# Gate and up tiles of a feed-forward chunk multiplied together, alternating between two PSUM banks

## The chip, the cores and the metric

The kernel runs on one core of a Trainium2 chip. The metric is the device time of one execution in microseconds (us), from the first to the last instruction with what lies around them. The engines that matter here are TensorE (PE in the profile, its weight loads PEld), ScalarE (ACT), VectorE (DVE) and SyncE (SP), which issues the loads of the weights.

## The reference, cut to what matters

The program is a four-layer block followed by a two-layer block over 256 tokens of width 1024, in fp32. Between attention, convolution and gating stages stand 12 feed-forward stages, all of this form (8 in the first block, 4 in the second, where gate and up lie side by side in one matrix):

```
D_MODEL = 1024;  D_FF = 2816;  SEQ = 256
x = x + 0.5 * (silu(rms_norm(x, g) @ w_gate) * (rms_norm(x, g) @ w_up)) @ w_down
```

## The kernel before

**Tiles.** Every weight matrix is read in tiles of 128 partitions x 2048 fp32 values, 1 MB each, 543 in all. A tile goes through three buffers of one slot number: `raw` (filled by a DMA), `w_hi` (ScalarE's rounding of raw to fp32r, L511) and `w_lo` (VectorE's raw minus w_hi, L835). There are RING = 3 slots; tile n uses slot n mod 3. Each product is made of three fp32r matmuls (`matmul3`, L1466 to L1468): high by high, high by low, low by high.

**A feed-forward stage.** The 2816 inner columns are cut in 11 chunks of 256. A chunk has a gate tile and an up tile (8 slices of 128 rows by 256 columns: 2 x 8 x 3 = 48 matmuls each, of 256 output columns, into one of the four `up` banks per tile) and a down tile (2 x 2 x 2 x 3 = 24 matmuls of 512 output columns, into the four `acc` banks, six into one bank and then six into the next). The order of tiles in a stage, the same on all engines, is: gate 0, up 0, gate 1, up 1, down 0, gate 2, up 2, down 1, ..., gate 10, up 10, down 9, down 10. A norm stage stands before each, and TensorE fills part of it with 18 matmuls on constants.

**What sets the order.** The order on each engine is written out, and semaphores tie them:

- TensorE, `ffn` and `gate_up`: before each tile it waits for `lo_ready` (one count per tile, from L835) and for a free bank (`bank_free`). The last matmul of a tile increments `tile_used`. A down tile also waits for `hlo_ready`, the low part of the product of its chunk.
- ScalarE, `ffn` / `chunk`: it waits for `tile_used` of the gate tile n, converts tile n+3 (`w_hi`, L511), does silu of the gate's bank (L571), waits for `tile_used` of the up tile n+1, converts tile n+4, makes the high part of the product (L564), waits for the down tile, converts its successor.
- VectorE, `ffn` / `chunk`: it waits for `tile_used` and `hi_ready` and makes `w_lo` of tile n+3, the same for tile n+4, then gate times up (L934), releases the two banks, makes the low part of the product (L924), then `w_lo` of the down tile's successor.
- SyncE loads tile n+3 into `raw` as soon as `w_lo` of tile n is made.

The first two and the last two tiles of a stage need one more remark. A stage begins with two chunks without a down tile between them, so up 1 (tile 3) takes the slot of gate 0 (tile 0). A stage ends with two down tiles; down 10 (tile 32) takes the slot of gate 10 (tile 29). At the very first stage, tile 0 is converted before the norm's outputs and tiles 1 and 2 after them.

Of the kernel before, what the change touches and what calls it, by code (L numbers as in the profile page):

```python
# [14 lines left out]
P = 128  # L15
TOK = 256
NT = TOK // P
D = 1024
KD = D // P
# [3 lines left out]
RING = 3  # L23
CW = 256
# [88 lines left out]
def build(nc, A, out, plan=None):  # L113
    plan = plan or full_plan()
    with ExitStack() as ctx:
        def sb(name, shape, dt=F32):
            return ctx.enter_context(nc.sbuf_tensor(name, shape, dt))

        def sem(name):
            return ctx.enter_context(nc.semaphore(name))  # L120
# [5 lines left out]
        w_hi = [sb(f"w_hi{i}", [P, TILE], F32R) for i in range(RING)]  # L126
        w_lo = [sb(f"w_lo{i}", [P, TILE], F32R) for i in range(RING)]

        xT_hi = sb("xT_hi", [P, KD, TOK], F32R)
        xT_lo = sb("xT_lo", [P, KD, TOK], F32R)  # L130
# [102 lines left out]
        up = [ctx.enter_context(nc.psum_tensor(f"up{i}", [P, 512], F32)) for i in range(4)]  # L233
# [8 lines left out]
        tile_used = sem("tile_used")  # L242
# [82 lines left out]
        def tview(buf, nk, n):  # L325
            return buf[:, 0:nk * n].rearrange("p (k n) -> p k n", k=nk)
# [1132 lines left out]
        def _(pe):  # L1459
# [4 lines left out]
            def matmul3(ps, lh, ll, rh, rl, start, stop):  # L1464

                pe.matmul(ps, lh, rh, start=start, stop=False)  # L1466
                pe.matmul(ps, lh, rl, start=False, stop=False)  # L1467
                return pe.matmul(ps, ll, rh, start=False, stop=stop)  # L1468

            def take_bank():  # L1470

                if credit[0]:
                    credit[0] -= 1
                else:
                    pe.wait_ge(bank_free, seen.next(bank_free))
                banks[0] += 1
                return (banks[0] - 1) % 4
# [6 lines left out]
            def up_matmuls(n, b):  # L1484

                wh, wl = tview(w_hi[n % RING], KD, CW), tview(w_lo[n % RING], KD, CW)
                for m in range(2):
                    for k in range(KD):
                        if k % 2 == 0:
                            next_pair()  # L1490
                        last = matmul3(up[b][:, m * TOK:(m + 1) * TOK], wh[:, k, m * P:(m + 1) * P],
                                       wl[:, k, m * P:(m + 1) * P], xT_hi[:, k, :], xT_lo[:, k, :],
                                       k == 0, k == KD - 1)
                last.then_inc(tile_used, 1)
# [46 lines left out]
            def next_pair():  # L1541

                if pairs_to_come[0]:
                    pe.wait_ge(xlo_ready, seen.next(xlo_ready))
                    pairs_to_come[0] -= 1
# [17 lines left out]
            def down(n, c, start, stop):  # L1563
                pe.wait_ge(lo_ready, seen.next(lo_ready))
                pe.wait_ge(hlo_ready, seen.next(hlo_ready))
                down_matmuls(n, hT_hi[:, c % 2], hT_lo[:, c % 2], start, stop)
# [116 lines left out]
            def ffn(s, n0):  # L1683
                def gate_up(n, c, b, loop=False):
                    for j in range(2):
                        pe.wait_ge(lo_ready, seen.next(lo_ready))
                        if loop:
                            pe.wait_ge(bank_free, seen.next(bank_free))
                        else:
                            assert take_bank() == (b + j) % 4  # L1690
                        up_matmuls(n + j, (b + j) % 4)

                b = banks[0] % 4
                gate_up(n0, 0, b)
                gate_up(n0 + 2, 1, b + 2)
                down(n0 + 4, 0, True, False)
                with pe.Fori(0, 4) as i:
                    seen.enter(i, [(lo_ready, 6), (bank_free, 4), (hlo_ready, 2)])
                    gate_up(n0 + 5, 2, b, True)
                    down(n0 + 7, 1, False, False)  # L1700
                    gate_up(n0 + 8, 3, b + 2, True)
                    down(n0 + 10, 2, False, False)
                    seen.leave(4)
                banks[0] += 16
                gate_up(n0 + 29, 10, b)
                down(n0 + 31, 9, False, False)
                down(n0 + 32, 10, False, True)
# [293 lines left out]
            for k in range(KD):  # L2001
                last = pe.transpose(up[3][:, k * G_ROWS:(k + 1) * G_ROWS], g_rows[:, k * P:(k + 1) * P],
                                    ident[0:G_ROWS, 0:G_ROWS])
# [191 lines left out]
```

## Time and profile before

| | |
|---|---|
| device time, median of 2 runs | 3684.26 us (3683.72 to 3684.81) |
| span of the profiled execution | 3684.0 us |
| TensorE busy | 3532.3 us (96%), 24279 matmuls, as many weight loads |
| VectorE busy | 1845.2 us (50%) |
| ScalarE busy | 1549.9 us (42%) |
| DMA | 576.08 MB, mean 156 GB/s; a 1 MB tile lands 4.8 to 5.2 us after its issue |
| mean granted TensorE clock | 0.966 of full speed |

The profiled execution lies within 0.3 us of the median of the runs, so it can stand for them. Busy time of TensorE is the union of matmuls that overlap in their pipeline: a matmul of 256 columns is shown with 0.28 us and one of 512 with 0.39 us, while the next begins before it ends. How fast it goes is read from the distance between starts. A group `line engine operation out<-in` names the buffer without its number, so `up` stands for any of four banks.

### The profile page before, as it was taken

How to read it: one execution, taken by the hardware profiler on the slowest of the kernel's cores; microseconds unless marked ns; L12 is line 12 of the kernel's file. 1: busy time of each engine (PE TensorE's matmuls, PEld its weight loads, DVE VectorE, ACT ScalarE, POOL GpSimd, SP SyncE). 2: the span in 40 equal slices, each digit the busy share in tenths (PEclk: the TensorE clock that was granted, in tenths of full speed). 3: DMA queues.
4: the chain of work that ended last, by engine and by line, in shares of the span. 5: the costliest groups of instructions: out<-in, count | busy, mean ns of one | idle time of the engine just before them, and what ended most of it. 6: DMA issues, size and time to landing. Idle time of an engine off the chain costs nothing.

```text
span 3684.0 us, 57759 instructions
## 1 busy us (share of the span) xinstructions
PE 3532.3 (96%) x24279; PEld 3261.1 (89%) x24279; DVE 1845.2 (50%) x2276; ACT 1549.9 (42%) x1836; POOL 161.6 (4%) x253
## 2 busy tenths in 40 slices
PE   8999999859999999999999999999999999999998
PEld 8999999748999899998999899878998998878997
DVE  4455454564454554444554545534545545434544
ACT  4344444334443443433343344355444443455443
POOL 0000000020000000000000000032000000131000
PEclk9999999979999999999999999879999999789999
DMA  6554555414555445555455455513454455413552
GB/s 210 184 166 166 185 168 184 148 35 152 184 170 183 165 149 188 164 184 171 156 171 182 148 183 174 164 35 104 163 186 156 162 189 158 127 49 113 191 184 101
DMA packets 452308, 576.08 MB, mean 156 GB/s; under 512 B 44650, under 2 KB 393937, under 8 KB 452013
## 3 DMA queue, kind: packets, MB, share of 16 engines
q1 hardware_dynamic: 449612, 566.71, 46.7%
q0 software_dynamic: 2384, 6.63, 0.6%
q8 instruction: 124, 2.03, 0.2%
q10 hardware_dynamic: 144, 0.35, 0.0%
q14 instruction: 44, 0.35, 0.0%
HBM read 571.53 MB, written 1.08 MB: 155 GB/s over the span
## 4 chain that ended last, share of the span: by engine, by line
PE 89%; DVE 7%; ACT 3%; issue 1%; DMA 0%; DVEq 0%; POOL 0%; SPq 0%; ACTq 0%; POOLq 0%
PE up L1466 20%; PE up L1468 19%; PE up L1467 19%; PE acc L1466 7%; PE acc L1467 7%; PE acc L1468 7%; DVE w_lo L835 2%; PE acc L1535 2%; ACT w_hi L511 2%; PE acc L1585 1%; PE up L1858 1%; PE up L1526 1%; PE acc L1592 1%; PE acc L1586 1%; DVE xT_lo L867 0%
## 5 line engine op out<-in xcount | busy, mean ns | idle before, releaser
L835 DVE TENSOR_TENSOR w_lo<-raw,w_hi 128x2048 fp32r<-128x2048 f32 x543 | 1244.4, 2292 | 1371.7 <-ACT w_hi L511 1368.8
L511 ACT ACTIVATE w_hi<-raw 128x2048 fp32r<-128x2048 f32 x543 | 1038.0, 1913 | 1262.5 <-PE up L1468 1206.1
L1466 PE MATMUL up<-xT_hi,w_hi 128*128 128x256 f32 x5392 | 1535.1, 285 | 16.6 <-DVEq L1315 10.2
L1467 PE MATMUL up<-xT_lo,w_hi 128*128 128x256 f32 x5392 | 1530.3, 284 | 0.0
L1468 PE MATMUL up<-xT_hi,w_lo 128*128 128x256 f32 x5392 | 1530.2, 284 | 0.0
L1466 PEld LDWEIGHTS up<-xT_hi,w_hi 128*128 128x128 f32 x5392 | 1039.3, 193 | 30.2 <-issue 18.7
L1467 PEld LDWEIGHTS up<-xT_lo,w_hi 128*128 128x128 f32 x5392 | 1039.3, 193 | 4.6
L1468 PEld LDWEIGHTS up<-xT_hi,w_lo 128*128 128x128 f32 x5392 | 1039.2, 193 | 0.0
L1466 PE MATMUL acc<-w_hi,hT_hi 128*128 128x512 f32 x1216 | 476.3, 392 | 15.7 <-DVE hT_lo L924 15.7
L1467 PE MATMUL acc<-w_lo,hT_hi 128*128 128x512 f32 x1216 | 474.7, 390 | 0.0
L1468 PE MATMUL acc<-w_hi,hT_lo 128*128 128x512 f32 x1216 | 473.2, 389 | 0.0
L1466 PEld LDWEIGHTS acc<-w_hi,hT_hi 128*128 128x128 f32 x1216 | 228.8, 188 | 65.3 <-issue 21.6
L564 ACT ACTIVATE hT_hi<-prod 128x512 fp32r<-128x512 f32 x144 | 91.0, 632 | 433.9 <-DVE prod L934 392.7
L1468 PEld LDWEIGHTS acc<-w_hi,hT_lo 128*128 128x128 f32 x1216 | 228.3, 188 | 48.6
L1467 PEld LDWEIGHTS acc<-w_lo,hT_hi 128*128 128x128 f32 x1216 | 228.9, 188 | 42.0
L924 DVE TENSOR_TENSOR hT_lo<-prod,hT_hi 128x512 fp32r<-128x512 f32 x144 | 99.8, 693 | 100.9 <-ACT hT_hi L564 100.9
L1466 PE MATMUL up<-w_hi,xT_hi 128*128 128x512 f32 (+3 forms) x292 | 103.2, 353 | 19.0 <-DVEq L1088 11.4
L2038 POOL TENSOR_SCALAR units<-units,rsum 128x256 f32<-128x256 f32 x80 | 67.2, 851 | 1069.8 <-DVE rsum L1026 1069.8
L523 ACT ACTIVATE xT_hi<-acc,gains 128x256 fp32r<-128x256 f32 x163 | 68.4, 471 | 88.6 <-PE acc L1535 76.7
L605 ACT ACTIVATE units<-units,nmax 128x256 f32<-128x256 f32 (+1 forms) x192 | 80.5, 421 | 55.5 <-DVE nmax L1018 51.2
L1468 PE MATMUL up<-w_hi,xT_lo 128*128 128x512 f32 (+3 forms) x292 | 102.4, 351 | 0.0
L1467 PE MATMUL up<-w_lo,xT_hi 128*128 128x512 f32 (+3 forms) x292 | 102.4, 351 | 0.0
(282 smaller groups left out, 2535.1 us busy)
## 6 DMA issues: line engine op xcount, KB each, us to landing
raw<-in_ffn_gate SPq DMA_DIRECT2D x88, 1024.0 KB, 5.1
raw<-in_ffn_up SPq DMA_DIRECT2D x88, 1024.0 KB, 5.2
raw<-in_ffn_down SPq DMA_DIRECT2D x88, 1024.0 KB, 4.8
raw<-in_ffn_wi SPq DMA_DIRECT2D x88, 1024.0 KB, 5.0
raw<-in_ffn_wo SPq DMA_DIRECT2D x44, 1024.0 KB, 4.8
raw<-in_w_in SPq DMA_DIRECT2D x44, 1024.0 KB, 5.0
raw<-in_conv_w_in SPq DMA_DIRECT2D x24, 1024.0 KB, 5.1
raw<-in_w_branch SPq DMA_DIRECT2D x12, 1024.0 KB, 5.0
```

The lines of the kernel that those rows point to most:

```text
L511: nc.scalar.activation(w_hi[n % RING][:], raw[n % RING][:], ACT.Copy).then_inc(hi_ready, 1)
L523: last = nc.scalar.activation(dst[:, k, :], src[k // 2][:, (k % 2) * TOK:(k % 2 + 1) * TOK], ACT.Copy, scale=g)
L564: nc.scalar.activation(hT_hi[:, par], prod[:].rearrange("p (k n) -> p k n", k=2), ACT.Copy).then_inc(hhi_ready, 1)
L605: last = nc.scalar.activation(S[b][:, lo:hi], S[b][:, lo:hi], ACT.Exp, bias=nmax[b][:, i:i + 1], scale=-1.0, accum_out=esum[b][:, i:i + 1])
L835: nc.vector.tensor_tensor(w_lo[n % RING][:], raw[n % RING][:], w_hi[n % RING][:].bitcast(F32), ALU.subtract).then_inc(lo_ready, 1)
L924: nc.vector.tensor_tensor(hT_lo[:, c % 2], prod[:].rearrange("p (k n) -> p k n", k=2), hT_hi[:, c % 2].bitcast(F32), ALU.subtract).then_in ...
L1466: pe.matmul(ps, lh, rh, start=start, stop=False)
L1467: pe.matmul(ps, lh, rl, start=False, stop=False)
L1468: return pe.matmul(ps, ll, rh, start=False, stop=stop)
L1526: pe.matmul(up[banks[0] % 4][:, 0:P], ident, ident, start=True, stop=True)
L1535: last = pe.matmul(acc[k // 2][:, (k % 2) * TOK + t * P:(k % 2) * TOK + (t + 1) * P], x[:, t, k * P:(k + 1) * P], diag[:, t, :], start=Tru ...
L2038: last = pool.tensor_scalar(S[b][:, lo:hi], S[b][:, lo:hi], rsum[b][:, t:t + 1], factors[t], ALU.mult, ALU.mult if factors[t] is not None ...
```

## The change

In `gate_up` the two waits (for the tile and for the bank) are now both done first, for the gate tile and for the up tile. Then one loop runs over the 2 column halves, the 8 slices and the 3 products, and in it over the two tiles: every matmul of the gate tile is followed by the same one of the up tile, in the neighbouring bank. The last matmul of each tile increments `tile_used`, so both increments come from the last two matmuls of the pair. All 12 feed-forward stages use it; the convolution, gating and attention stages keep `up_matmuls`.

```diff
@@ gate_up, after the waits of both tiles @@
-                        up_matmuls(n + j, (b + j) % 4)
+                    wh = [tview(w_hi[(n + j) % RING], KD, CW) for j in range(2)]
+                    wl = [tview(w_lo[(n + j) % RING], KD, CW) for j in range(2)]
+                    last = [None, None]
+                    for m in range(2):
+                        cols = slice(m * P, (m + 1) * P)
+                        for k in range(KD):
+                            if k % 2 == 0:
+                                next_pair()
+                            for i in range(3):
+                                for j in range(2):
+                                    last[j] = pe.matmul(up[(b + j) % 4][:, m * TOK:(m + 1) * TOK],
+                                                        (wh, wh, wl)[i][j][:, k, cols],
+                                                        (xT_hi, xT_lo, xT_hi)[i][:, k, :],
+                                                        start=k == 0 and i == 0, stop=k == KD - 1 and i == 2)
+                    for j in range(2):
+                        last[j].then_inc(tile_used, 1)
```

The orders of ScalarE, VectorE, SyncE and GpSimd are the same in both programs. On TensorE two places show what moves. `lo_ready` is the tile's `w_lo`, `xlo_ready` a pair of slices of the norm's output; in the changed kernel every matmul of a pair has the line L1701.

TensorE, first stage, before: where the gate tile of chunk 0 ends and its up tile begins.

```order
L1468 MATMUL up<-xT_hi,w_lo 128x256
L1466 MATMUL up<-xT_hi,w_hi 128x256 [waits lo_ready]
L1467 MATMUL up<-xT_lo,w_hi 128x256
L1468 MATMUL up<-xT_hi,w_lo 128x256
L1466 MATMUL up<-xT_hi,w_hi 128x256
L1467 MATMUL up<-xT_lo,w_hi 128x256
```

TensorE, first stage, changed: the first matmuls of chunk 0.

```order
L1701 MATMUL up<-xT_hi,w_hi 128x256 [waits xlo_ready,lo_ready]
L1701 MATMUL up<-xT_hi,w_hi 128x256
L1701 MATMUL up<-xT_lo,w_hi 128x256 x2
L1701 MATMUL up<-xT_hi,w_lo 128x256 x2
L1701 MATMUL up<-xT_hi,w_hi 128x256 x2
L1701 MATMUL up<-xT_lo,w_hi 128x256 x2
L1701 MATMUL up<-xT_hi,w_lo 128x256 x2
```

The wait for the up tile stood 48 matmuls after the chunk's start and now stands at it, together with the gate tile's; `x2` is one matmul of the gate and one of the up tile.

TensorE, first stage, before: where chunk 0 ends and chunk 1 begins. The wait is for gate 1 alone; that for up 1 stands 48 matmuls further down.

```order
L1467 MATMUL up<-xT_lo,w_hi 128x256
L1468 MATMUL up<-xT_hi,w_lo 128x256
L1466 MATMUL up<-xT_hi,w_hi 128x256 [waits lo_ready]
L1467 MATMUL up<-xT_lo,w_hi 128x256
L1468 MATMUL up<-xT_hi,w_lo 128x256
L1466 MATMUL up<-xT_hi,w_hi 128x256
```

TensorE, first stage, changed: the same place.

```order
L1701 MATMUL up<-xT_hi,w_hi 128x256 x2
L1701 MATMUL up<-xT_lo,w_hi 128x256 x2
L1701 MATMUL up<-xT_hi,w_lo 128x256 x2
L1701 MATMUL up<-xT_hi,w_hi 128x256 [waits lo_ready]
L1701 MATMUL up<-xT_hi,w_hi 128x256
L1701 MATMUL up<-xT_lo,w_hi 128x256 x2
L1701 MATMUL up<-xT_hi,w_lo 128x256 x2
```

The one wait now counts up to `w_lo` of up 1, tile 3, whose slot the matmul just ahead of it was the last to read for tile 0.

## Rows read from the trace of the kernel before

**Rows 1.** the page: busy times, engines' shares of the chain of waits

```profile
PE 3532.3 (96%) x24279; PEld 3261.1 (89%) x24279; DVE 1845.2 (50%) x2276; ACT 1549.9 (42%) x1836; POOL 161.6 (4%) x253
...
PE 89%; DVE 7%; ACT 3%; issue 1%; DMA 0%; DVEq 0%; POOL 0%; SPq 0%; ACTq 0%; POOLq 0%
```

**Rows 2.** timeline of TensorE: start us, us, instruction, [idle before <-releaser]; up and down tiles

```profile
1006.68 0.28 PE L1468 MATMUL up<-xT_hi,w_lo 128*128 128x256 f32 x1
1006.80 0.40 PE L1466 MATMUL acc<-w_hi,hT_hi 128*128 128x512 f32 x1
...
1007.97 0.39 PE L1468 MATMUL acc<-w_hi,hT_lo 128*128 128x512 f32 x1
1008.19 0.39 PE L1466 MATMUL acc<-w_hi,hT_hi 128*128 128x512 f32 x1
...
1012.27 0.28 PE L1466 MATMUL up<-xT_hi,w_hi 128*128 128x256 f32 x1
...
1017.90 0.28 PE L1468 MATMUL up<-xT_hi,w_lo 128*128 128x256 f32 x1
1018.02 0.28 PE L1466 MATMUL up<-xT_hi,w_hi 128*128 128x256 f32 x1
```

**Rows 3.** timeline of ScalarE in the same chunk

```profile
1001.33 1.92 ACT L511 ACTIVATE w_hi<-raw 128x2048 fp32r<-128x2048 f32 x1 [3.92 <-PE up L1468]
1003.14 0.58 ACT L571 ACTIVATE gate<-up 128x512 f32<-128x512 f32 x1
1007.00 1.92 ACT L511 ACTIVATE w_hi<-raw 128x2048 fp32r<-128x2048 f32 x1 [3.28 <-PE up L1468]
1011.88 0.63 ACT L564 ACTIVATE hT_hi<-prod 128x512 fp32r<-128x512 f32 x1 [2.96 <-DVE prod L934]
1012.47 1.92 ACT L511 ACTIVATE w_hi<-raw 128x2048 fp32r<-128x2048 f32 x1
```

**Rows 4.** timeline of VectorE in the same chunk

```profile
1003.27 2.29 DVE L835 TENSOR_TENSOR w_lo<-raw,w_hi 128x2048 fp32r<-128x2048 f32 x1 [3.54 <-ACT w_hi L511]
1008.95 2.29 DVE L835 TENSOR_TENSOR w_lo<-raw,w_hi 128x2048 fp32r<-128x2048 f32 x1 [3.39 <-ACT w_hi L511]
1011.16 0.68 DVE L934 TENSOR_TENSOR prod<-gate,up 128x512 f32<-128x512 f32 x1
1012.54 0.69 DVE L924 TENSOR_TENSOR hT_lo<-prod,hT_hi 128x512 fp32r<-128x512 f32 x1 [0.70 <-ACT hT_hi L564]
```

**Rows 5.** timeline of TensorE: first matmul of the last down tile of a stage

```profile
1047.41 0.47 PE L1466 MATMUL acc<-w_hi,hT_hi 128*128 128x512 f32 x1 [1.01 <-DVE hT_lo L924]
```

**Rows 6.** timelines, first stage: conversions of tiles 1 and 2; first matmul of tile 0

```profile
24.14 4.50 DVE L835 TENSOR_TENSOR w_lo<-raw,w_hi 128x2048 fp32r<-128x2048 f32 x2 [0.92 <-ACT w_hi L511]
...
21.19 0.36 PE L1466 MATMUL up<-xT_hi,w_hi 128*128 128x256 f32 x1
```

**Rows 7.** timelines elsewhere: matmuls of TensorE that ended an idle time, and one conversion

```profile
1291.18 1.23 PE L1675 MATMUL up<-arena,xn 128*128 128x128 f32 x6 [3.62 <-DVE xn L1176]
...
2325.91 2.29 DVE L835 TENSOR_TENSOR w_lo<-raw,w_hi 128x2048 fp32r<-128x2048 f32 x1 [1.22 <-ACT w_hi L511]
...
2328.26 0.39 PE L1466 MATMUL up<-xT_hi,w_hi 128*128 128x256 f32 x1 [3.00 <-DVE w_lo L835]
2328.48 0.28 PE L1467 MATMUL up<-xT_lo,w_hi 128*128 128x256 f32 x1
...
3378.56 0.36 PE L1466 MATMUL up<-xT_hi,w_hi 128*128 128x256 f32 x1 [3.10 <-DVEq L1315]
```

**Rows 8.** windows: busy us (instructions) of PE, PEld, DVE, ACT, POOL; clock; DMA share, GB/s

```profile
2325.00:2328.00 3.00, 0.26 (x3) 0.00 (x0) 2.09 (x1) 3.00 (x3) 0.00 (x0) 1.00 0.00 0
2329.00:2333.00 4.00, 4.00 (x23) 4.00 (x23) 3.74 (x3) 0.40 (x1) 0.00 (x0) 0.57 1.14 213
3378.00:3382.00 4.00, 3.44 (x29) 3.47 (x30) 2.65 (x2) 0.00 (x0) 0.00 (x0) 1.00 0.23 80
1047.40:1051.00 3.60, 3.59 (x16) 2.96 (x17) 2.53 (x2) 0.94 (x1) 0.00 (x0) 1.00 0.67 233
```

## The prediction

> **What bounds the kernel now.** I read the page first: TensorE is busy for 3532 of 3684 us and is 89% of the chain of waits, the other engines and the DMAs hardly stand in it [rows 1]. So what counts is how long TensorE idles and how far apart its matmuls start. Next the timeline of TensorE through one chunk of a feed-forward stage. An up tile from 1012.27 to 1018.02 us takes 5.75 us, 48 matmuls at 0.120 us; a down tile from 1006.80 to 1012.27 us takes 5.47 us, 24 matmuls at 0.228 us [rows 2]. Nothing idles between tiles. Then ScalarE and VectorE in the same chunk: a conversion is 1.92 us on ScalarE and 2.29 us on VectorE, and the second starts 1.94 to 1.95 us after the first [rows 3, 4]. A tile is thus ready some 4.3 us after its slot comes free, and in the order of before it is wanted two tiles later, after 11.2 us or more. That slack of about 7 us is why TensorE never waits.
>
> **What stays.** Matmuls and weight loads are as many as before, as are the conversions, and their order on ScalarE, VectorE and SyncE. Only 12 x 22 x 48 = 12,672 matmuls are dealt out differently, and two waits and one release per chunk move.
>
> **The alternation itself: 0.** Before, the step from the gate's bank to the up's bank is 1017.90 to 1018.02 us, 0.12 us like any other; the step from one acc bank to the next is 1007.97 to 1008.19, 0.22 us like the others of a down tile [rows 2]. A step with the same weights (L1466 to L1467) and one with new weights keep the same distance. So neither a change of bank nor one of weights costs or gives anything that shows. At the full clock of 2.4 GHz, 256 columns are 0.107 us, so 0.013 us of the 0.120 is something else; if all of it hung on the bank, alternating could save 0.013 us or cost as much again. Times 12,672 that is 169 us either way. These are the bounds; I take 0, since the rows with a bank change show exactly that.
>
> **The wait of a steady chunk: 1.48 us.** Now both slots of a pair come free at its end, call it E (in the rows: last matmul 1006.68 + 0.28 = 1006.96), and both successors must be ready when the one down tile behind it is done. That down tile ends, as TensorE's next slot, at 1012.27, E + 5.31. Step by step, with distances of [rows 3, 4]:
> - ScalarE starts the first conversion at E + 0.04 (1007.00) and the silu 1.81 later (1001.33 to 1003.14), E + 1.85.
> - The silu takes 0.58 and the next conversion begins some 0.55 after it (0.59 behind the slightly longer 0.63 at 1011.88): E + 2.40.
> - VectorE starts its second conversion 1.95 later, E + 4.35, done at E + 6.64; its first ran from E + 1.98 to E + 4.27.
> - TensorE starts 0.05 after such an end (a conversion from 2325.91, done at 2328.20, lets the matmul at 2328.26 go [rows 7]) and the first step after an idle time is 0.22 instead of 0.12 [rows 7].
>
> So 6.64 + 0.05 - 5.31 + 0.10 = **1.48 us**, of which 0.55 is the silu, which ran beside the up tile's matmuls before and now stands between the two conversions. The Trainium skill ("Perfetto Trace Analysis", Optimizing Tensor Performance) says matmul groups should rotate through PSUM banks so that one group's evacuation runs beside the next group's matmuls; the change gives up that overlap inside a chunk, and the trace of before shows it (silu at 1003.14 beside the up tile). By that rule alone the wait would be the silu's 0.55 a chunk; by the rows it is the whole of the second tile's conversion. Chunks 2 to 10 have this wait: 9 x 1.48 = 13.3 us a stage.
>
> **Chunk 1: 4.58 us.** No down tile stands before it, and up 1 takes the slot of gate 0. It is ready at E + 4.27, TensorE starts at E + 4.32 instead of E - 0.16 (1006.80 against 1006.96), plus 0.10.
>
> **The last down tile: 2.36 us.** It waits for the product of chunk 10, and already idled 1.01 us for it [rows 5]. The product is made behind VectorE's second conversion (1008.95 to 1011.16, 2.21 us [rows 4]). Before, that conversion started at E + 1.99, now at E + 4.35; everything behind it moves by 2.36.
>
> **The first stage: 5.29 us once.** Tile 0 started at 21.19; `w_lo` of tile 1 is made from 24.14, done at 26.43, so TensorE starts at 26.48 [rows 6]. In later stages tiles 0 and 1 are made before the norm ends.
>
> Sum of waits: 12 x (13.3 + 4.58 + 2.36) + 5.3 = 12 x 20.26 + 5.3 = **248 us**.
>
> **Covers.** The product of a chunk now ends at about E + 8.6 (from 1012.54 + 0.69, moved by 2.36), and its down tile comes 18 us after E; the down tile's successor is converted behind it, by about E + 12, wanted at E + 18; banks come free at E + 7.2, wanted a whole chunk later. The loads of a pair are issued at E + 4.3 and E + 6.6 and need about 5 us each; they are wanted at E + 18. All of these stay hidden with 5 us or more to spare.
>
> **The clock.** TensorE is granted 1.0 in the feed-forward stages. Elsewhere seven idle times of 2.9 to 4.1 us stand in the trace that began at full clock, the first of 3.62 at 1291.18, the last of 3.10 at 3378.56 [rows 7]. After six of them the clock went to its lower level (1.2 GHz), after the last one it did not. One of the six: idle 3.00 to 2328.26, then 4.00 us with a clock of 0.57 and 23 matmuls, where 33 fit at 0.12; 10 x 0.12 = 1.2 us lost [rows 7, 8]. After 3378.56 the clock stays 1.00, and so it does after the 1.01 us before 1047.41 [rows 5, 8]. The change makes 25 idle times of that length (12 of 4.3, 12 of 1.01 + 2.36 = 3.4, one of 5.3). 6/7 x 25 = 21 falls at 1.3 us: **27 us**, with bounds 0 (none) and 65 (all, each twice as long). The 108 short waits of 1.3 us of idling resemble the 1.01 us one, and cost nothing here. The Trainium skill ("TensorE: Matmul & The Clock Gate", Why this matters for your kernels) warns of idle gaps between bursts of matmuls because the clock falls back; six of seven rows agree with it. By the rule taken without exception all 25 would fall, and the term would be 32.
>
> **Sum.** 3684 + 248 + 27 + 0 = **3959 us**, +7.5%. The profiled span and the median of the runs differ by 0.3 us, so it is the same against either.
>
> **Rivals.**
> - *The bank was part of the pace.* If two neighbouring matmuls into one bank hold each other up, alternating wins up to 0.013 us each: 3959 - 169 = 3790 us at the most. Against it: the steps with a bank change in [rows 2] are no shorter. 6%.
> - *The bank change costs when it comes every time.* Up to 0.013 us more: 4128 us. Against it: the same steps. 4%.
> - *The clock falls in the short waits too.* 108 more falls at 1.3 us: about 4100 us. For it: they repeat every 18 us. Against it: 1.01 us passed without a fall [rows 5, 8], and TensorE works for 17 of 18 us. The Trainium skill ("TensorE: Matmul & The Clock Gate", A second HAM failure mode: psum-queue depth-cycling) tells of a kernel that cycled through PSUM banks, idled briefly between groups and saw its clock swing; no row here shows it for idle times near 1 us. 5%.
> - *Two banks let two matmuls run at once* (the other side). Then the distance could go below the 0.107 us that the columns of one need. It decides from 275 / 12,672 = 0.022 us a matmul, a distance of 0.098, where the waits are just paid; from 0.104 the time is within 2%. At 0.090 us it gives 3959 - 380 = 3579 us. Against it: no step of the trace with a change of bank goes below 0.12. 2%.
> - *The change does not do what it says.* The order of the built program shows the pairs and the joint wait, so I give this nothing.
>
> **How the numbers follow.** The forecast has 83%, and its own range is 3920 (no fall of the clock, waits 0.1 us shorter) to 4005 (bound of the clock, waits 0.1 us longer). To leave out no more than 2 in 10 the range reaches a little towards the first rival: 3900 to 4005. About 2% (74 us) is what a measurement of this kernel tells from no change. Slower by over 2% holds in all cases but the fourth rival: 98%. That one is split between faster and same, 1% each.
>
> **What the changed profile would show.** VectorE's `w_lo` stands in the waits of TensorE's paired line some 120 times, 1.2 to 1.3 us each in chunks 2 to 10 and 4.3 us in chunk 1, about 190 us together; the chunk repeats every 18.4 us instead of 17.0; the idle time before a last down tile is 3.4 us; pairs run at 0.120 us a matmul; busy time of VectorE and ScalarE is unchanged, and the clock is low in about 20 short stretches more. I would be wrong if the pairs ran at another distance, if TensorE's wait ended on a DMA or a bank, or if the chunk's period were not 18.4 us.

## The result and the profile after

The changed kernel took 3974.41 us (median of 2 runs, 3974.22 to 3974.61) against 3684.26 us: ratio 1.078, 95% interval 1.0765 to 1.080. The profiled execution has a span of 3972.7 us, 288.7 us more than the one before, and is what the numbers below come from.

The page of the changed kernel, parts 1, 4 and 5; the first four lines answer to [rows 1], the fifth is one of the three groups of the paired line, with its idle time at the end.

```profile
span 3972.7 us, 57771 instructions
...
PE 3608.1 (91%) x24279; PEld 3293.0 (83%) x24279; DVE 1846.8 (46%) x2276; ACT 1530.8 (39%) x1836; POOL 160.9 (4%) x253
...
PE 69%; DVE 14%; ACT 10%; issue 6%; DMA 0%; ACTq 0%; DVEq 0%; POOL 0%; SPq 0%; POOLq 0%
PE up L1701 40%; DVE w_lo L835 10%; ACT w_hi L511 7%; PE up L1466 6%; PE up L1468 5%; PE up L1467 5%; PE acc L1466 2%; PE acc L1535 2%; PE acc L1467 2%; PE acc L1468 2%; ACT gate L571 1%; PE acc L1585 1%; PE up L1873 1%; PE up L1526 1%; PE acc L1592 1%
...
L1701 PE MATMUL up<-xT_hi,w_hi 128*128 128x256 f32 x4224 | 873.9, 289 | 186.6 <-DVE w_lo L835 186.6
```

As many matmuls and loads as before. TensorE's share of the chain fell from 89% to 69%, VectorE's rose to 14% and ScalarE's to 10%: the two conversions now stand in the path. The view of waits of TensorE says how long and how often (us in total, times, longest):

```profile
PE up L1701 <- DVE w_lo L835: 186.6, 121, 5.1
PE acc L1466 <- DVE hT_lo L924: 41.8, 15, 3.2
...
PE acc L1535 <- DVE diag L896: 5.5, 5, 3.0
```

The first line did not exist before; 121 is 12 stages x 10 chunks and the first stage's start. The second stood at 15.7 us in 15 times; the third, the norm's, is for later and was the same (5.5 us in 5 times).

The timelines of one steady chunk, VectorE, ScalarE and TensorE (start us, us, instruction, idle before and who ended it), answering to [rows 2 to 4]:

```profile
1085.28 4.58 DVE L835 TENSOR_TENSOR w_lo<-raw,w_hi 128x2048 fp32r<-128x2048 f32 x2 [8.46 <-ACT w_hi L511]
1089.77 0.68 DVE L934 TENSOR_TENSOR prod<-gate,up 128x512 f32<-128x512 f32 x1
...
1103.71 4.58 DVE L835 TENSOR_TENSOR w_lo<-raw,w_hi 128x2048 fp32r<-128x2048 f32 x2 [8.46 <-ACT w_hi L511]
```

```profile
1083.32 1.92 ACT L511 ACTIVATE w_hi<-raw 128x2048 fp32r<-128x2048 f32 x1 [8.83 <-PE up L1701]
1085.15 0.58 ACT L571 ACTIVATE gate<-up 128x512 f32<-128x512 f32 x1
1085.62 1.91 ACT L511 ACTIVATE w_hi<-raw 128x2048 fp32r<-128x2048 f32 x1
```

```profile
1082.92 0.40 PE L1701 MATMUL up<-xT_hi,w_lo 128*128 128x256 f32 x2
1083.16 0.40 PE L1466 MATMUL acc<-w_hi,hT_hi 128*128 128x512 f32 x1
...
1094.16 0.40 PE L1701 MATMUL up<-xT_hi,w_lo 128*128 128x256 f32 x2
1094.40 0.40 PE L1701 MATMUL up<-xT_hi,w_hi 128*128 128x256 f32 x2
...
1106.84 0.39 PE L1468 MATMUL acc<-w_hi,hT_lo 128*128 128x512 f32 x1
1108.42 0.50 PE L1701 MATMUL up<-xT_hi,w_hi 128*128 128x256 f32 x2 [1.19 <-DVE w_lo L835]
```

The pair ends at 1083.32; ScalarE converts, does the silu, converts again; VectorE's two conversions (x2, one line for two instructions) run from 1085.28 to 1089.86 without a gap; the down tile's last matmul starts at 1106.84 in the next round and the next pair only at 1108.42, after 1.19 us of idling. The chunk repeats every 18.43 us (1085.28 to 1103.71). Two matmuls of a pair, one into each bank, start every 0.24 us (1094.16, 1094.40), 0.120 us each, as before. The two long waits, at a stage's end and start, and the first stage's:

```profile
1143.79 0.39 PE L1468 MATMUL acc<-w_hi,hT_lo 128*128 128x512 f32 x1
1147.36 0.47 PE L1466 MATMUL acc<-w_hi,hT_hi 128*128 128x512 f32 x1 [3.18 <-DVE hT_lo L924]
...
1178.51 0.47 PE L1701 MATMUL up<-xT_hi,w_hi 128*128 128x256 f32 x2 [4.37 <-DVE w_lo L835]
```

```profile
28.34 0.77 PE L1701 MATMUL up<-xT_hi,w_hi 128*128 128x256 f32 x2 [5.10 <-DVE w_lo L835]
```

Windows behind five idle times (busy us and instructions of each engine, granted clock, DMA share, GB/s), answering to [rows 8]: behind a short one, behind the two long ones above, behind another stage's long wait before chunk 1, and behind the one last down tile where the clock stayed.

```profile
1090.00:1094.00 4.00, 4.00 (x33) 4.00 (x34) 2.19 (x3) 2.44 (x2) 0.00 (x0) 1.00 1.08 361
1147.40:1151.40 4.00, 4.00 (x12) 3.14 (x13) 2.89 (x2) 0.94 (x2) 0.00 (x0) 0.62 0.87 273
1178.50:1182.50 4.00, 3.99 (x21) 4.00 (x22) 3.31 (x3) 0.63 (x1) 0.00 (x0) 0.57 0.73 221
2285.90:2290.90 5.00, 5.00 (x24) 5.00 (x25) 3.35 (x3) 0.63 (x1) 0.00 (x0) 0.50 0.80 265
2474.60:2478.60 4.00, 4.00 (x18) 3.29 (x19) 3.03 (x3) 0.94 (x2) 0.00 (x0) 1.00 0.81 258
```

The clock is 1.00 after the short wait, 0.57 to 0.62 after the long ones, 0.50 over all 5 us after another, and 1.00 after the one at 2474.6. The mean granted clock of the whole span, from the view of cores:

```profile
core 0: 3972.7 us, clock 0.954
```

It was 0.966 before. The lower level is half of the full clock, so twice the missing share, times the span, is the time at the lower level: about 250 us before and 365 us now, some 115 us more (the clock is given to three digits, which leaves 4 us open on each).

### The profile page after: what moved, and what is told of

Read it like the earlier page. It is cut to its first block, busy times and chain, and to the rows that moved or that the text cites. A ratio compares the mean times of both kernels' runs of the same rounds, so it can differ in the third digit from the quotient of the medians.

```text
span 3972.7 us, 57771 instructions
## 1 busy us (share of the span) xinstructions
PE 3608.1 (91%) x24279; PEld 3293.0 (83%) x24279; DVE 1846.8 (46%) x2276; ACT 1530.8 (39%) x1836; POOL 160.9 (4%) x253
## 4 chain that ended last, share of the span: by engine, by line
PE 69%; DVE 14%; ACT 10%; issue 6%; DMA 0%; ACTq 0%; DVEq 0%; POOL 0%; SPq 0%; POOLq 0%
PE up L1701 40%; DVE w_lo L835 10%; ACT w_hi L511 7%; PE up L1466 6%; PE up L1468 5%; PE up L1467 5%; PE acc L1466 2%; PE acc L1535 2%; PE acc L1467 2%; PE acc L1468 2%; ACT gate L571 1%; PE acc L1585 1%; PE up L1873 1%; PE up L1526 1%; PE acc L1592 1%
## 5 line engine op out<-in xcount | busy, mean ns | idle before, releaser
L1701 PE MATMUL up<-xT_hi,w_hi 128*128 128x256 f32 x4224 | 873.9, 289 | 186.6 <-DVE w_lo L835 186.6
L1701 PEld LDWEIGHTS up<-xT_hi,w_hi 128*128 128x128 f32 x4224 | 667.8, 195 | 233.5 <-issue 153.6
L1701 PE MATMUL up<-xT_lo,w_hi 128*128 128x256 f32 x4224 | 859.9, 285 | 0.0
L1701 PE MATMUL up<-xT_hi,w_lo 128*128 128x256 f32 x4224 | 859.9, 285 | 0.0
L1701 PEld LDWEIGHTS up<-xT_lo,w_hi 128*128 128x128 f32 x4224 | 668.0, 195 | 0.0
L1701 PEld LDWEIGHTS up<-xT_hi,w_lo 128*128 128x128 f32 x4224 | 667.9, 194 | 0.0
L1466 PE MATMUL up<-xT_hi,w_hi 128*128 128x256 f32 x1168 | 339.3, 291 | 16.5 <-DVEq L1315 10.2
L1467 PE MATMUL up<-xT_lo,w_hi 128*128 128x256 f32 x1168 | 334.8, 287 | 0.0
L1468 PE MATMUL up<-xT_hi,w_lo 128*128 128x256 f32 x1168 | 334.6, 287 | 0.0
L1466 PEld LDWEIGHTS up<-xT_hi,w_hi 128*128 128x128 f32 x1168 | 228.7, 196 | 25.9 <-issue 18.6
L1467 PEld LDWEIGHTS up<-xT_lo,w_hi 128*128 128x128 f32 x1168 | 228.7, 196 | 0.4
L1468 PEld LDWEIGHTS up<-xT_hi,w_lo 128*128 128x128 f32 x1168 | 228.4, 196 | 0.0
```

The lines of the kernel that those rows point to most:

```text
L1701: last[j] = pe.matmul(up[(b + j) % 4][:, m * TOK:(m + 1) * TOK], (wh, wh, wl)[i][j][:, k, cols], (xT_hi, xT_lo, xT_hi)[i][:, k, :], start= ...
```

## The experiments

All ran beside the kernel before on the same chip, whose medians on the three chips used were 3680 to 3686 us. "E" is, as in the prediction, the end of a pair. What differs is told against the changed kernel (3974 us) or the kernel before.

**1. Joint wait and release without alternating.** The order of the matmuls is the old one.

```diff
 # after both tiles' waits
-for m, k, product: for j in (gate, up): matmul(tile j)
+for j in (gate, up): up_matmuls(tile j)
+# both tile_used increments on the last two matmuls of the up tile
```

> The matmuls of gate and up tile in the old order, one tile after the other, but with the new joint wait (both tiles ready before the first matmul) and the new joint release (both slots reported used by the last two matmuls of the pair). Theory (the waits are the whole loss, alternating the banks costs nothing): 3974 us within 3 us, chunk period 18.4 us, 120-odd waits of the pair for w_lo, 187 us together. Rival (the alternation itself has a price or a gain of up to 0.013 us per matmul): up to 169 us less or more than 3974.

Measured: 3973.9 us (3972.3 to 3974.9), within 0.5 us of the changed kernel. TensorE's waits are the same ones (the line number is that of the old matmul in this file):

```profile
PE up L1493 <- DVE w_lo L835: 186.5, 121, 5.1
PE acc L1466 <- DVE hT_lo L924: 41.7, 15, 3.2
```

So the whole 290 us comes with the joint wait and release; what a change of bank at each of 12,672 matmuls costs or wins is within the 4 us by which the medians of the kernel before beside them differ (3684.3 and 3680.6 us), 0.0003 us each.

**2. The joint wait alone.** Each tile is released by its own last matmul.

```diff
 # after both tiles' waits
-paired matmuls, both tile_used at the end
+for j in (gate, up): up_matmuls(tile j)   # tile_used with each tile's last matmul
```

> Old order, joint wait at the start of a pair, each tile released by its own last matmul as before. Theory: gate's slot comes free 5.75 us before the pair's end E, so its successor is ready before E; up's successor is ready at E + 4.3, before the down tile ends at E + 5.3; only the first stage waits (5.3 us and one fall of the clock): 3684 + 7 = 3691 us. Rival (the joint wait is what costs): near 3900 us.

Measured: 3688.9 us (3685.3 to 3699.8), ratio 1.003 (1.0015 to 1.0045), 8 us above the kernel before on that chip. What is left of waits for w_lo in the feed-forward stages is the first stage's. The wait for the product is as before:

```profile
PE acc L1466 <- DVE hT_lo L924: 15.7, 15, 1.4
...
PE up L1493 <- DVE w_lo L835: 5.1, 1, 5.1
```

**3. The joint release alone.** Each tile is waited for on its own.

```diff
 wait(gate); gate's 48 matmuls
-    last of gate: tile_used + 1
 wait(up); up's 48 matmuls
+    last but one of up: tile_used + 1
     last of up: tile_used + 1
```

> Old order, each tile waited for on its own, both slots released by the last two matmuls of the up tile. Theory: the gate's successor is ready at E + 4.3 against E + 5.3, the up's at E + 6.6 against E + 11: no wait in the chunks. Only the product of the last chunk is late by 2.3 us behind the second conversion, 12 x (2.2 + a fall of the clock of 1.6) = 46 us: 3730 us. Rival (the joint release is what costs): near 3900 us.

Measured: 3741.1 us (3731.1 to 3746.3), ratio 1.0164 (1.0136 to 1.0192). The profiled execution had a span of 3729.4 us, as expected; the median lies 11 us higher. The times of the four runs follow their mean granted clocks: 3731.1 us at 0.960, 3737.6 at 0.959, 3744.5 at 0.957, 3746.3 at 0.956. A clock lower by 0.004 over 3740 us is 15 us, the whole of their spread. The kernel before did the same there, from 3672.1 us at 0.969 to 3691.8 at 0.964. So the 11 us go with time at the lower level that one execution has and another has not; what decides it is not shown. The only wait that grew is the last down tile's, to what it is in the changed kernel:

```profile
PE acc L1466 <- DVE hT_lo L924: 41.7, 15, 3.2
```

Neither half costs more than some 60 us alone; together they cost 290. In the chunks a late release is harmless while the up tile is wanted a whole tile later, and an early wait is harmless while the gate's slot comes free a whole tile earlier.

**4. The silu out of the way.**

```diff
 # ScalarE, chunk
 consumed(n)                      # convert the gate's successor
-silu(gate); consumed(n + 1)      # convert the up's successor
+consumed(n + 1); silu(gate)
```

> The changed kernel with ScalarE's silu of the gate behind both conversions instead of between them. By the prediction's reading (0.55 of the 1.48 us is the silu) the wait of a chunk falls by 0.55 us: 3974 - 60 = 3914 us. Rival (VectorE is the bound: its second conversion can't begin before its first ends, 2.2 us after E + 1.98): it falls by 0.1 to 0.16 us a chunk, 3957 to 3964 us.

Measured: 3960.2 us (3958.1 to 3963.2), 14 us less, as the rival had it. ScalarE and VectorE in a steady chunk:

```profile
1096.63 3.72 ACT L511 ACTIVATE w_hi<-raw 128x2048 fp32r<-128x2048 f32 x2 [8.83 <-PE up L1701]
1100.25 0.57 ACT L572 ACTIVATE gate<-up 128x512 f32<-128x512 f32 x1
```

```profile
1098.58 4.49 DVE L835 TENSOR_TENSOR w_lo<-raw,w_hi 128x2048 fp32r<-128x2048 f32 x2 [8.46 <-ACT w_hi L511]
...
1116.91 4.49 DVE L835 TENSOR_TENSOR w_lo<-raw,w_hi 128x2048 fp32r<-128x2048 f32 x2 [8.46 <-ACT w_hi L511]
```

ScalarE's two conversions are now back to back (x2, 3.72 us), but VectorE takes 4.49 us for its two without waiting for ScalarE between them, only 0.09 us less than in the changed kernel, and the chunk repeats every 18.33 us instead of 18.43. VectorE is the bound of the wait.

**5. Matmuls on constants in the long waits.**

```diff
+if chunk == 1: 18 x matmul(up[b][:, 0:128], ident, ident)      # before the wait for w_lo
 ...
+14 x matmul(up[b + 2][:, 0:128], ident, ident)                 # a free bank, before the last down tile
 down(n0 + 32, 10, False, True)
```

> The changed kernel with matmuls on constants put into its two kinds of long wait: 18 before chunk 1 of each stage (4.2 us at 0.23 us each, beside a wait of 4.5) and 14 before the last down tile (3.3 us beside 3.4). They touch a free bank that the next chunk overwrites. The waits stay. Theory (the falls of the clock after the long idle times cost 1.4 to 2.7 us each, 24 of them, 43 us together): 3974 - 41 = 3933 us, and only the fall at the first stage's start is left in the feed-forward stages. Rival (the falls cost what the prediction took, 1.3 us each): 3974 - 30 = 3944 us. Rival (nothing hangs on them): 3974 us.

Measured: 3923.9 us (3918.7 to 3931.3), 50 us less. The fill and the wait behind it, in the second stage's chunk 1, and the mean clock:

```profile
356.68 4.18 PE L1689 MATMUL up<-consts 128*128 128x128 f32 x36
361.21 0.47 PE L1706 MATMUL up<-xT_hi,w_hi 128*128 128x256 f32 x2 [0.35 <-DVE w_lo L835]
```

```profile
core 0: 3926.1 us, clock 0.968
```

The 18 matmuls (two rows each, x36) don't make the pair wait longer: 4.18 + 0.35 = 4.53 us stand where 4.37 us of idling and the last 0.16 us of a matmul's end stood. The clock is 0.968, 251 us at the lower level, what it was before the change. So the falls of the clock are worth some 46 us (the difference of the two spans, 3972.7 and 3926.1, within each of which the clock is known), 1.7 times the 27 us that the prediction took.

**6. The last chunk's product first.**

```diff
 # ScalarE and VectorE, chunk 10 only
-convert the up tile's successor; product of gate and up
+product of gate and up; convert the up tile's successor
```

> The changed kernel, but in chunk 10 ScalarE and VectorE make the product of gate and up before they convert the up tile's successor. Theory: the product is as early as in the kernel before, the last down tile starts 2.2 us earlier, the idle time is 1.0 us again and no clock falls there: 3974 - 12 x (2.2 + 1.6) = 3929 us. Rival (the last down tile's delay is given back in the norm that follows): 3974 us or little less.

Measured: 3945.6 us (3942.7 to 3948.0), 29 us less and not 45. The last down tile's wait is back where it was, but another has grown, TensorE's for the norm's diag, which was 5.5 us in 5 times in both kernels:

```profile
PE acc L1545 <- DVE diag L901: 20.2, 14, 3.0
PE acc L1476 <- DVE hT_lo L929: 15.1, 15, 1.4
```

```profile
1140.09 4.49 DVE L840 TENSOR_TENSOR w_lo<-raw,w_hi 128x2048 fp32r<-128x2048 f32 x2 [1.18 <-ACT w_hi L511]
1144.50 2.48 DVE L922 SCALAR_TENSOR_TENSOR x<-acc,x 128x512 f32<-128x512 f32 x4
```

VectorE makes two conversions (x2, to 1144.58) before it turns to the residual; the down tile's banks are ready earlier, and the norm can't start sooner. Part of the gain is given back there; experiment 11 measures how much. The falls of the clock at the last down tiles are gone, 11 in the trace of the changed kernel; but all the time at the lower level, summed as in the next section, costs only 11 us less, because other stretches of it lasted longer in this execution.

**7. Alternating from chunk 2 on.**

```diff
 def gate_up(n, c, b, loop):
+    if c < 2: the old gate_up, tile by tile; return
```

> The changed kernel with chunks 0 and 1 of each stage multiplied tile by tile as before, alternating only in chunks 2 to 10. Theory: no wait in chunk 1 (12 x 4.6), none in chunk 2, whose up tile takes a slot that chunk 1 frees after its gate tile... its gate and up successors are ready at E + 4.3 (12 x 1.45), none in the first stage (5.3), and the 13 falls of the clock behind these waits gone (26): 3974 - 104 = 3870 us. Rival (the chunk's wait hangs on something built up over the stage, so that chunk 2 still waits): 3887 us.

Measured: 3873.0 us (3865.8 to 3875.5), 101 us less. TensorE waits 96 = 12 x 8 times, so chunk 2 does not wait either, and none is longer than 1.4 us:

```profile
PE up L1710 <- DVE w_lo L835: 115.0, 96, 1.4
```

**8. Alternating with the up tile 12 matmuls behind.**

```diff
-wait(gate); wait(up); for q in 0..47: gate(q), up(q)
+wait(gate); gate(0..11); wait(up); for q in 12..47: gate(q), up(q - 12)
+up(36..47)      # tile_used with each tile's own last matmul
```

> Alternating kept, but the up tile runs 12 matmuls (1.44 us) behind the gate tile and is waited for only then; each tile is released by its own last matmul. 72 of a pair's 96 matmuls still change bank each time. Theory: the gate's slot comes free 1.44 us earlier and the up tile is wanted 1.44 us later, so chunks 2 to 10 wait for nothing; chunk 1 still waits 1.7 us, the last down tile comes 0.9 us later than in the kernel before, the first stage loses 5.5: 3684 + 37 = 3721 us, up to 3730 with a few falls of the clock. Rival (alternating has a price of its own that the equality of the joint kernels hid): more than 3740 us.

Measured: 3721.3 us (3706.5 to 3725.5), 253 us less, ratio to the kernel before 1.010 (1.007 to 1.013). Of 121 waits for w_lo 13 are left, those of chunk 1 and of the first stage:

```profile
PE acc L1466 <- DVE hT_lo L924: 24.4, 15, 1.7
...
PE up L1707 <- DVE w_lo L835: 18.9, 13, 3.5
```

1.44 us of stagger between the two tiles removes nine waits in ten, with the banks still changing at 72 of 96 matmuls of a pair.

**9 and 10. Toward a faster kernel.** Both start from the kernel before, tile by tile. The first has the edit of 6. The second also moves one conversion of VectorE behind the norm's diag:

```diff
 # VectorE, end of a stage, in the second only
-split_lo(successor of down 9); residual; row scales; diag
+residual; row scales; diag; split_lo(successor of down 9)
```

> The kernel before (tile by tile), with only the order of chunk 10 changed: product of gate and up before the conversion of the up tile's successor. The 1.0 us wait of the last down tile goes: 12 x 1.3 = 15 us at most. But the two conversions then lie ahead of the residual, as in the changed kernel with the same edit (norm's wait for diag 20 us instead of 5.5). Theory: the residual starts at E + 9.6 instead of E + 9.8 and ends 0.85 us earlier: 12 x 0.85 = 10 us less than the kernel before on the same chip. Rival (all given back in the norm): no difference.

> As the kernel before, chunk 10 with the product first, and VectorE's conversion of the last but one tile's successor moved behind the norm's diag, where VectorE otherwise waits 2.1 us for ScalarE. Theory: nothing stands ahead of the residual, which follows the last down tile's matmuls: 12 x 1.25 = 15 us less than the kernel before. Rival (the moved conversion delays the norm's low parts by as much): 10 us or less.

Measured: 3683.4 us for the first, ratio 0.9994 (0.9981 to 1.0007), no difference; 3673.9 us for the second (3672.5 to 3677.8), ratio 0.9971 (0.9960 to 0.9982), 0.3% less than the kernel before and the lowest median here. Waits of TensorE in the first, then in the second:

```profile
PE acc L1545 <- DVE diag L901: 12.3, 14, 3.0
...
PE acc L1476 <- DVE hT_lo L929: 3.5, 3, 1.4
```

```profile
PE acc L1552 <- DVE diag L904: 6.4, 5, 3.7
...
PE acc L1483 <- DVE hT_lo L934: 3.5, 3, 1.4
```

In both the 12 waits for the product are gone (15.7 to 3.5 us). The first gains 12.2 us there and gives 6.8 back at the diag; most of what is left is lost to the clock, 0.963 instead of 0.966. In its trace three idle times of 1.9 to 2.0 us and one of 3.1 us are followed by a fall that in the trace of the kernel before were not. Eleven of its 12 runs have 0.963 or 0.964, the twelfth 0.970 and 3661.0 us; why is not shown. In the second the clock is 0.966 again. The moved conversion fits, but for some 0.4 us, in the time in which VectorE waited 2.1 us for ScalarE, and the 12 us lie between the 15 expected and the rival's 10. A gain of 0.3% is outside the interval of the noise, but far below the 2% that the prediction counts as a change.

**11. The same two edits in the changed kernel.**

> The changed kernel with both of these edits. With the first alone it took 3946 instead of the 3929 us expected, and TensorE's wait for the norm's diag had grown from 5.5 to 20 us. Theory (the two conversions ahead of the residual gave the gain back): the diag waits shrink to 5.5 us or less and the time is 3946 - 15 = 3931 us. Rival (something else in the norm): 3946 us.

Measured: 3933.5 us (3929.8 to 3939.5), 12 us less than with the product alone. The wait for the diag is 6.4 us again:

```profile
PE acc L1552 <- DVE diag L904: 6.4, 5, 3.7
```

So the conversions ahead of the residual took some 12 us of the 17 that experiment 6 fell short (12.0 between the two spans, 13.8 in the wait for the diag). The two ran on chips on which the kernel before differs by 5 us, so whether anything is left of the 17 stays open; the smaller gain in the clock (experiment 6) is the candidate that the traces show.

## Why the prediction was right, and by how much

The forecast was 3959 us, the result 3974. Step by step, from the trace of the changed kernel where no other source stands:

| step | predicted | measured |
|---|---|---|
| bank changes | 0 | 0 (experiment 1) |
| wait of chunks 2 to 10 | 108 x 1.48 = 160 us | 108 x 1.45 = 157 us (period 18.43 us against 16.98 before) |
| wait of chunk 1 | 12 x 4.58 = 55 us | 12 x 4.6 = 55 us (4.37 idle, 0.16 of the pipeline's end, 0.10 restart) |
| last down tile | 12 x 2.36 = 28 us | 12 x 2.17 = 26 us (3.18 - 1.01 idle) |
| first stage | 5.3 us | 5.3 us (5.10 idle, 0.2 beside it) |
| falls of the clock | 27 us | 45 us (the rest of 288.7; experiment 5: 46 us) |

**The mechanism** was the predicted one: early waits and late releases put both conversions in TensorE's path, and [rows 2 to 4] held nearly every distance that was needed. The waits came out at 243 us, within 5 of 248, because each conversion lasts the same in both kernels. That they came so close is in part luck: in the median of the 108 short waits the second conversion on ScalarE starts at E + 2.30 and not 2.40, so VectorE is done at E + 6.53 and not 6.64, but TensorE starts 0.13 us behind that and not 0.05. The waits were forecast 5 us too long and the clock 18 us too cheap; the total is 15 us off. The loads stayed hidden as forecast, although the median load of an up tile in the first block now lands 6.2 us after its issue instead of 5.2.

**The term that was mis-sized is the clock.** The prediction counted 21 falls at 1.3 us. In the trace's record of the granted clock 24 of the 25 long idle times are followed by one, where I took 6 in 7; and a fall cost more than the 1.2 us read off one window. The 23 matmuls of that window [rows 8] take in two that began before it, so 12 and not 10 are missing, 1.4 us. In the window at 1178.5 only 21 matmuls stand in 4 us where 33 fit, 12 x 0.12 = 1.4 us lost, and where the lower clock lasts beyond 5 us, as at 2285.9, 24 matmuls stand in place of 42, 2.1 us. Summed over the starts of the matmuls in these 24 stretches (how much each distance exceeds that at full clock) it is 43 us, 1.8 each; the remaining 2 of the 45 us are in stretches elsewhere. The upper bound of 65 covered it.

In 12 of the 24 the record shows the clock down before the idle time had ended, in the others up to 1.3 us after it. The rule of the Trainium skill ("TensorE: Matmul & The Clock Gate", Why this matters for your kernels) taken without exception gave 25 falls and 32 us: nearer in number, and still short in size. Behind the 108 short waits of some 1.2 us the record of the granted clock has no fall, so the rival with falls in the short waits is refuted. What the Trainium skill ("TensorE: Matmul & The Clock Gate", A second HAM failure mode: psum-queue depth-cycling) tells of another kernel does not show at these idle times of 1.2 us. Idle times of 1.9 to 2.0 us outside the feed-forward stages, which the prediction did not weigh, are mixed: of five that began at full clock, one was followed by a fall in the kernel before and three in the changed one.

**One sentence was wrong although the sum was right:** that 0.55 of the 1.48 us is the silu. Experiment 4 took it away and won 0.09 us a chunk. I had walked along ScalarE's path alone. VectorE's first conversion starts at E + 1.98, and what stands right behind a conversion starts 2.21 us after it [rows 4], so without the silu the second could begin at E + 4.19 instead of the E + 4.35 that I had put down: the silu could be worth 0.16 us at most. Measured, the first ends at E + 4.24 and the second starts there. The rule of the Trainium skill on rotating banks ("Perfetto Trace Analysis", Optimizing Tensor Performance) asks that one group's evacuation runs beside the next group's matmuls. The silu lost its place beside the up tile's matmuls and runs beside the down tile's instead (silu from 1085.15, down tile from 1083.16), so the overlap only moved; what the silu held up was 0.09 us a chunk and not 0.55.

**The rivals** on the bank, in both directions, and on two matmuls at once are refuted by experiment 1: the same time with and without alternating, and 0.120 us a matmul in both.

## What to carry to other kernels

With few slots, what an interleaving of two tiles costs was set here by when the slots are released and when the successors are wanted, not by the banks: the wait alone cost 8 us, the release alone 60 and both together 290, and a stagger of 12 matmuls gave 253 us back. When two paths lead to a wait, work out both ends before calling an instruction the cost. Idle times of TensorE of 3 to 5 us cost some 1.8 us beyond their length here, because the clock falls in or behind them; and whoever removes a wait should look at what the freed engine does next, since conversions ahead of the residual took 12 of the 45 us expected at the stages' ends.

## What the runs showed of the hardware

- Alternating fp32r matmuls of 256 columns between two PSUM banks, with a weight load for each, runs at 0.120 us a matmul, as does a run into one bank.
- Of 25 idle times of TensorE of 3.2 to 5.1 us at full clock, 24 were followed by a stretch at the lower level that cost 1.4 to 2.7 us; 108 of about 1.2 us were not. Matmuls on constants in them prevented all but the first stage's, whose wait had no fill.
- Of five idle times of 1.9 to 2.0 us that began at full clock, one was followed by the lower level in the kernel before and three in the changed one.
- The mean granted clock differs between executions of one kernel, and the time goes with it: the kernel before took 3672.1 us at 0.969 and 3691.8 us at 0.964 on one chip.
